# Fourier features kept as 130 mirrored columns instead of 256, and gate rows multiplied out of two fp32r parts instead of fp32

## The reference

```python
def fourier_mixer(h, w_o):
    B, S, D = h.shape
    hg = h.astype(jnp.float32).reshape(B, S, FOURIER_GROUPS, FOURIER_GROUP_DIM)   # 4 groups of 256
    f = jnp.fft.fftn(hg, axes=(1, 3), norm="ortho").real.astype(h.dtype)
    return f.reshape(B, S, D) @ w_o

# second_block, layer i (0: Fourier, 1: retention)
mod = c_act @ w_ada[i] + b_ada[i]
sh1, sc1, g1, sh2, sc2, g2 = jnp.split(mod, 6, axis=-1)
h = modulate(rmsnorm(x, norm_mix_g[i]), sh1, sc1)
x = x + g1[:, None, :] * fourier_mixer(h, w_fourier_out[j])      # or retention_mixer
h = modulate(rmsnorm(x, norm_ffn_g[i]), sh2, sc2)
x = x + g2[:, None, :] * swiglu(h, w_ffn_in[i], w_ffn_out[i])
```

## Time and profile before

| | |
|---|---|
| median of 3 runs | 1161.5 us (1161.35 to 1162.33) |
| the profiled execution's own time | 1163.92 us |
| its span, first to last instruction | 1161.8 us |
| granted TensorE clock, mean | 0.996 |
| TensorE busy | 1144.9 us, 99% |
| VectorE busy | 836.4 us, 72% |
| ScalarE busy | 537.9 us, 46% |
| HBM traffic | 223 GB/s over the span |

### The profile page before, as it was taken

How to read it: one execution, slowest core, us unless ns; L and a number is a source line. 1 busy time by engine, 2 the same in 40 slices (tenths; PEclk the granted TensorE clock), 3 DMA queues, 4 the chain that set the end, 5 groups by cost and what they waited for, 6 DMA issues and landing times.

```text
span 1161.8 us, 14068 instructions
## 1 busy us (share of the span) xinstructions
PE 1144.9 (99%) x5856; PEld 967.3 (83%) x5856; DVE 836.4 (72%) x965; ACT 537.9 (46%) x525; POOL 27.2 (2%) x51
## 2 busy tenths in 40 slices
PE   9999999999999999999999999999999999999997
PEld 7998998888788888888788888889877887888886
DVE  6789879977587668566777676479846857867754
ACT  6656456525553443555544343443332444444431
POOL 1000000000000000000000000000001000000000
PEclk9999999999999999999999999999999999999999
DMA  7854553456477778534367768368743654877751
GB/s 270 309 223 157 187 189 139 162 205 259 145 290 273 270 296 292 199 109 146 145 247 263 293 258 342 131 241 301 291 176 109 246 225 161 308 292 270 287 204 37
DMA packets 39071, 259.81 MB, mean 224 GB/s; under 512 B 4192, under 2 KB 6496, under 8 KB 8416
## 3 DMA queue, kind: packets, MB, share of 16 engines
q1 hardware_dynamic: 37392, 251.84, 58.8%
q0 software_dynamic: 1616, 7.08, 1.8%
HBM read 257.86 MB, written 1.05 MB: 223 GB/s over the span
## 4 chain that ended last, share of the span: by engine, by line
PE 89%; DVE 6%; ACT 2%; DMA 2%; issue 2%; POOL 0%; SPq 0%; POOLq 0%; ACTq 0%; DVEq 0%
PE pair L449 45%; PE pair L514 18%; PE pair L475 10%; PE pair L530 4%; PE tp L571 3%; DVE w_lo L1275 3%; PE tp L633 2%; PE tp L847 1%; DMA raw<-stream 1%; PE pair L786 1%; ACT w_hi L878 1%; PE tp L775 1%; DVE hb L1325 1%; PE tp L660 1%; PE tp L825 1%
## 5 line engine op out<-in xcount | busy, mean ns | idle before, releaser
L1275 DVE TENSOR_TENSOR w_lo<-raw,w_hi 128x2048 fp32r<-128x2048 f32 x180 | 409.2, 2287 | 100.2 <-ACT w_hi L878 99.4
L878 ACT ACTIVATE w_hi<-raw 128x2048 fp32r<-128x2048 f32 x180 | 344.0, 1915 | 224.6 <-DMA raw<-stream 129.7
L449 PE MATMUL pair<-w_hi,ht_lo 128*128 128x512 f32 x800 | 319.5, 399 | 5.8 <-DVE w_lo L1275 5.8
L449 PE MATMUL pair<-w_lo,ht_hi 128*128 128x512 f32 x800 | 312.4, 391 | 0.0
L449 PE MATMUL pair<-w_hi,ht_hi 128*128 128x512 f32 x800 | 312.2, 390 | 0.0
L449 PEld LDWEIGHTS pair<-w_hi,ht_lo 128*128 128x128 f32 x800 | 150.7, 188 | 38.5 <-DVE w_lo L1275 7.5
L449 PEld LDWEIGHTS pair<-w_lo,ht_hi 128*128 128x128 f32 x800 | 150.5, 188 | 32.1
L449 PEld LDWEIGHTS pair<-w_hi,ht_hi 128*128 128x128 f32 x800 | 150.9, 189 | 30.6 <-issue 1.2
L1284 DVE SCALAR_TENSOR_TENSOR raw<-raw,crow 128x1024 f32<-128x1024 f32 x112 | 132.3, 1218 | 0.6 <-DMA raw<-stream 0.6
L514 PE MATMUL pair<-w_hi,gt_lo 128*128 128x512 f32 x272 | 107.5, 395 | 0.5 <-DVE gt_lo L1351 0.3
L514 PE MATMUL pair<-w_lo,gt_hi 128*128 128x512 f32 x272 | 106.0, 390 | 0.0
(11 more groups left out here) (230 smaller groups left out, 1289.9 us busy)
## 6 DMA issues: line engine op xcount, KB each, us to landing
raw<-stream SPq DMA_DIRECT2D x237, 1024.0 KB, 4.9
xres<-x SPq DMA_DIRECT2D x2, 512.0 KB, 4.9
raw<-stream SPq DMA_DIRECT2D x4, 256.0 KB, 7.0
prow<-rows POOLq DMA_DIRECT2D x1, 1024.0 KB, 8.6
xres<-x POOLq DMA_DIRECT2D x2, 512.0 KB, 5.7
dt<-decay POOLq DMA_DIRECT2D x1, 1024.0 KB, 7.0
outT<-outb SPq DMA_DIRECT2D x4, 256.0 KB, 2.6
csr<-dft POOLq DMA_DIRECT2D x1, 768.0 KB, 4.7
```

What stands on the lines that cost most here:

```text
L449: mm = pe.matmul(pair[use % 2][:, t, :], a[:, 4 * c + k, t * P:(t + 1) * P], b[:, w % WS, k * 512:(k + 1) * 512], start=(c == 0 and k == 0 ...
L878: sc.activation(w_hi[:, w % WS, :], raw[:, n % RAW, :], ACT.Copy).then_inc(hi_done, 1)
L1275: v.tensor_tensor(w_lo[:, w % WS, :], raw[:, n % RAW, :], whi32[:, w % WS, :], ALU.subtract).then_inc(raw_done, 1)
```

## The change

Two things change, independent of each other.

**130 of 256 bins.** The input of the feature transform is real, so its cosine sum is the same at bin 256-j as at bin j, and its sine sum has the other sign. `features` now makes bins 0 to 129 of both (`HALF = 130`): the moving operand is two runs of 130 columns out of `cs`, 260 in all, and the copies to `tt_hi` and `tt_lo` are 260 columns wide. `tokens` makes as many matmuls of the same width as before: for m = 0 it takes bins 0 to 127 as stationary operand, for m = 1 bins 1 to 128, read as bins 255 down to 128, and there the sine table enters with the other sign (`cs` from column 256 instead of 512). The second half of each group's mixed features thereby stands in reversed order on the partitions, and the host reverses the rows of `fo` to match (`mirrored`).

**Gate rows in two fp32r parts.** `gate_diagonals` first copies the gate's eight columns to an fp32r tile, subtracts to get the low part (both with a wait on the step before), and writes high and low diagonals with one instruction each of 128 x 1024, whose two inputs are repeated by access pattern. `gate_rows` multiplies the ones, now of type fp32r, with the high and the low diagonals: four fp32r matmuls of 512 columns in place of two fp32 products. The other uses of `ones` stay fp32.

```diff
--- before.py
+++ after.py
@@ -27,6 +27,7 @@
 D = 1024
 KT = D // P
 FF = 2816
+HALF = 130
 FT = FF // P
 HEADS = 8
 HH = HEADS // 2
@@ -200,7 +201,8 @@
         xn = sb("xn", 164, [P, TT, D])
 
         idn = sb("idn", 172, [P, P])
-        ones = sb("ones", 172.5, [P, P])
+        ones_r = sb("ones", 172.5, [P, P], F32R)
+        ones = ones_r[:].bitcast(F32)
         col = sb("col", 173, [P, NCOL])
         mod = sb("mod", 173.875, [P, 112])
         moda = sb("moda", 174.375, [P, 5, 8])
@@ -239,13 +241,14 @@
         prow = sb("prow", 185.25, [P, 2, D])
         praw = sb("praw", 193.25, [P, 2, S])
         pt = [sb("pt_hi", 195.25, [P, 2, S], F32R), sb("pt_lo", 197.25, [P, 2, S], F32R)]
-        dg = sb("dg", 88, [P, KT, P])
-        dgb = sb("dgb", 185.25, [P, KT, P])
+        dg = [sb("dg_hi", 88, [P, KT, P], F32R), sb("dg_lo", 92, [P, KT, P], F32R)]
+        dgb = [sb("dgb_hi", 185.25, [P, KT, P], F32R), sb("dgb_lo", 189.25, [P, KT, P], F32R)]
+        modr = sb("modr", 174.3125, [P, 2, KT], F32R)
         prod = sb("prod", 92, [P, 2, TT, 256])
         csr = sb("csr", 112, [P, 2, 768])
         cs = [sb("cs_hi", 185.25, [P, 2, 768], F32R), sb("cs_lo", 191.25, [P, 2, 768], F32R)]
         grow = [sb("grow0", 201.25, [P, D]), sb("grow1", 197.25, [P, D])]
-        tt = [sb("tt_hi", 112, [P, TT, 4, 512], F32R), sb("tt_lo", 134, [P, TT, 4, 512], F32R)]
+        tt = [sb("tt_hi", 112, [P, TT, 4, 2 * HALF], F32R), sb("tt_lo", 134, [P, TT, 4, 2 * HALF], F32R)]
         qr = sb("qr", 112, [P, RH, 2, S])
         kr = sb("kr", 120, [P, RH, 2, S])
         vr = sb("vr", 128, [P, TT, RH * RV])
@@ -590,8 +593,11 @@
                 for half in range(2):
                     k = JOB[name] + half
                     claim(k)
-                    pe.matmul(tp[k % BANKS][:], ones[:], dg[:, 4 * half:4 * half + 4, :].rearrange("p a b -> p (a b)"),
-                              start=True, stop=True).then_inc(tp_done, 1)
+                    for part in range(2):
+                        mm = pe.matmul(tp[k % BANKS][:], ones_r[:],
+                                       dg[part][:, 4 * half:4 * half + 4, :].rearrange("p a b -> p (a b)"),
+                                       start=(part == 0), stop=(part == 1))
+                    mm.then_inc(tp_done, 1)
 
             def hidden(name, jobs, j):
 
@@ -772,7 +778,9 @@
                     claim(k)
                     for d in range(2):
                         for n, (a, b) in enumerate(passes(ht, cs)):
-                            mm = pe.matmul(tp[k % BANKS][:], a[:, 2 * gr + d, t * P:(t + 1) * P], b[:, d, 0:512],
+                            mm = pe.matmul(tp[k % BANKS][:, 0:2 * HALF].rearrange("p (a b) -> p a b", a=2),
+                                           a[:, 2 * gr + d, t * P:(t + 1) * P],
+                                           b[:, d, 0:2 * S].rearrange("p (a b) -> p a b", a=2)[:, :, 0:HALF],
                                            start=(d == 0 and n == 0), stop=(d == 1 and n == 2))
                     mm.then_inc(tp_done, 1)
 
@@ -784,8 +792,8 @@
                         for part in range(2):
                             for o, (a, b) in enumerate(passes(tt, cs)):
                                 mm = pe.matmul(mixed(gr)[:, m * S:(m + 1) * S],
-                                               a[:, t, gr, part * S + m * P:part * S + (m + 1) * P],
-                                               b[:, t, 2 * part * S:(2 * part + 1) * S],
+                                               a[:, t, gr, part * HALF + m:part * HALF + m + P],
+                                               b[:, t, (2 - m) * part * S:((2 - m) * part + 1) * S],
                                                start=(t == 0 and m == 0 and part == 0 and o == 0),
                                                stop=(t == 1 and m == 1 and part == 1 and o == 2))
                     if t:
@@ -1155,7 +1163,9 @@
 
             def dft_his(name, t, groups):
                 for gr in groups:
-                    hi(JOB[name] + gr, tt[0][:, t, gr, :])
+                    k = JOB[name] + gr
+                    act.wait_ge(tp_done, k + 1)
+                    hi(k, tt[0][:, t, gr, :], tp[k % BANKS][:, 0:2 * HALF])
 
             for t in range(TT):
                 if t == 0:
@@ -1390,8 +1400,12 @@
             def gate_diagonals(at_col, read=None, dg=dg):
                 if read is not None:
                     dve.wait_ge(tp_done, read)
-                for m in range(KT):
-                    ins = v.tensor_scalar(dg[:, m, :], idn[:], mod[:, at_col + m:at_col + m + 1], None, ALU.mult)
+                gate = mod[:, at_col:at_col + KT]
+                link(v.tensor_copy(modr[:, 0, :], gate))
+                link(v.tensor_tensor(modr[:, 1, :], gate, as_f32(modr[:, 0, :]), ALU.subtract))
+                for part in range(2):
+                    ins = v.tensor_tensor(dg[part][:], idn[:].unsqueeze(1).to_broadcast([P, KT, P]),
+                                          as_f32(modr[:, part, :]).unsqueeze(2).to_broadcast([P, KT, P]), ALU.mult)
                 ins.then_inc(dg_done, 1)
 
             def hidden_los(jobs, j):
@@ -1691,7 +1705,7 @@
             def dft_los(name, t, groups):
                 for gr in groups:
                     k = JOB[name] + gr
-                    lo(k, tt[1][:, t, gr, :], tt32[:, t, gr, :], tp[k % BANKS][:])
+                    lo(k, tt[1][:, t, gr, :], tt32[:, t, gr, :], tp[k % BANKS][:, 0:2 * HALF])
 
             for t in range(TT):
                 wait_evac(dve, USE["pleg"] + t)
@@ -1885,6 +1899,11 @@
 
         return w.T.reshape(-1, 2, P, D).transpose(0, 2, 1, 3).reshape(-1, P, 2 * D)
 
+    def mirrored(w):
+
+        a = w.reshape(-1, 2, P, D)
+        return np.stack([a[:, 0], a[:, 1, ::-1]], axis=1).reshape(D, D)
+
     def outer(w):
         return w.reshape(-1, 2, P, D).transpose(0, 2, 1, 3).reshape(-1, P, 2048)
 
@@ -1901,7 +1920,7 @@
         "zi": deep(z["zi"], 512), "zg": deep(z["zg"], 512), "ga": deep(z["ga"], 512), "gb": deep(z["gb"], 512),
         "wa": outer(get("w_a")[0]), "wb": outer(get("w_b")[0]), "wout": outer(get("w_out")[0]),
         "ffn0": gate_up(get("w_gate")[0], get("w_up")[0]), "down0": outer(get("w_down")[0]),
-        "ple": outer(get("w_ple")[0]), "pleg": outer(get("w_ple_gate")[0]), "fo": outer(get("w_fourier_out_2")[0]),
+        "ple": outer(get("w_ple")[0]), "pleg": outer(get("w_ple_gate")[0]), "fo": outer(mirrored(get("w_fourier_out_2")[0])),
         "ffn1": gate_up(fi[0][:, :FF], fi[0][:, FF:]), "down1": outer(fo[0]),
         "rq": deep(ri[:, 0:1024], 256), "rk": deep(ri[:, 1024:2048], 256),
         "rva": deep(ri[:, 2048:3072], 512), "rvb": deep(ri[:, 3072:4096], 512), "rg": deep(ri[:, 4096:6144], 512), "ro": outer(get("w_ret_out_2")[0]),
```

## The result

The changed kernel takes 1155.52 us in the median of 4 runs (1154.07 to 1156.12), the kernel before 1161.42 us (1161.29 to 1162.33): a ratio of 0.9946, 95% interval 0.9928 to 0.9963. Forecast were 1154.9 us and a range of 1153.0 to 1158.0. The profiled execution took 1156.12 us with a span of 1154.0; the one of before took 1163.92 and 1161.8.

The account below looks back on a forecast made before the run. TensorE was taken as the bound, busy 1144.9 of 1161.8 us, with VectorE close behind in the Fourier stage. Fourier stage 4.2 plus three sets of gate rows 2.4 gave 6.6 us off 1161.5: 1154.9 us, range 1153.0 to 1158.0.

Parts of the forecast that it names:

- 3, transposes of tile 1: Fourier stage: TensorE waits 0.3 us for the norm, then transposes tile 1 from 522.05 instead of 524.1.
- 4, VectorE scales tile 1: Fourier stage: scaling starts 1.9 us earlier, at 522.75, so tile 1 is ready at 527.6 instead of 529.51.
- step 1: `features` of tile 0: three groups take 2.5 us, no stall for the first low part, fourth group ends at 518.8.
- step 6: `features` of tile 1 starts at 527.6, its fourth group runs to 530.95; `tokens` of tile 1 gains 4.2 us.
- Step 7: `tokens` of tile 1: fourth low part ready at 535.2, needed at 535.27; `fo` starts at 536.8, gain 4.2 us.
- step 5: After the first gate rows TensorE waits about 1 us for tile 1's split; the 0.81 us of `rows0` is worth nothing.
- (a): `features`: cost of a moving operand in two runs of 130; taken as 0.122 us, from above 0.43.
- (b): 48 of 96 `tokens` matmuls: stationary operand one column off; taken as costing nothing, from above 5.1 us.
- The rivals that hung on them: In `features`, short runs lose the fp32r rate: 1168.5 us, chance 0.04; in `tokens`, shifted weights are dearer: 1160.0, chance 0.05.
- that of the diagonals: Rival at the four gate-row places: VectorE's dearer diagonals reach the path, up to 4.8 us back, 1155 to 1159.7; chance 0.03.
- full payout: Rival in the Fourier stage: nothing is absorbed, 5.0 us there, 1153.3 us in all; chance 0.06.
- the greater absorption: Rival: thin margins miss or copies gain less, Fourier stage gives only 2 to 3 us, 1156 to 1157.5; chance 0.09.

Follow-up runs that it names:

- rows_only: Kernel before with only the gate rows in two fp32r parts, 256 bins kept: 1159.87 us, ratio 0.9978.
- rows0_fp32: Changed kernel with the first set of gate rows put back to fp32 products and eight diagonals: 1154.19 us, ratio 0.9932.
- fourier_only: Kernel before with only the 130-bin part of the change, gate rows left in fp32: 1158.56 us, ratio 0.9969.
- diagonals_twice: Changed kernel with each pair of diagonals written twice on VectorE: 1154.9 us, ratio 0.9933.
- changed_again: The changed kernel itself, unaltered, timed again on another chip: median 1154.2 us, ratio 0.9934.
- keep_busy: Changed kernel with eight small fp32 products filling a 2.3 us TensorE wait in the first feed-forward layer: median 1154.03 us, ratio 0.9928.

## Why the prediction was right

Times relative to the start of the first `features`, as predicted and as measured:

| step | predicted | measured |
|---|---|---|
| 1, TensorE's stall ahead of the fourth group | none | 0.19 |
| 1, fourth group starts | 2.48 | 2.48 |
| 3, transposes of tile 1 | 6.48 | 6.40 |
| 4, VectorE scales tile 1 | 7.18 | 7.09 |
| 5, TensorE's wait behind the gate rows | 1 us | 0.69 (0.87 from start to start) |
| 6, second `features` | 12.03 | 11.96 |
| 6, its fourth group | 14.63 | 14.50 |
| 6, `tokens` of tile 1 | 15.38 | 15.33 |
| 7, gain of the stage | 4.2 | 4.31 |

- **The prices** held: 0.122 us for 260 columns (measured 0.122), 0.39 and 0.42 us for the copies (0.39 and 0.42 to 0.43), 0.91 for the gate rows (0.91 and 0.92), 1.22 for a diagonal (1.22 to 1.23).
- **Two errors cancelled in steps 1 and 6.** The prediction gave each `features` some 0.3 us at its start, out of the chain's sums. TensorE's records show 0.10 more than the pace there (0.22 from the first start to the second), and the rest is a stall ahead of the fourth group, for the first low part: 0.19 us at tile 0, where step 1 says "No stall", and 0.26 at tile 1 (529.83 against 529.57 by the pace), where step 6 has 0.1. The start of the fourth group came out right because VectorE sets it. Step 7 had more room than its 0.07 us: the fourth low part ends at 534.20 + 0.42 = 534.62, and TensorE starts on the last group at 534.95.
- **What step 5 said of `rows0`** was shown by three runs: nothing when cheapened alone (`rows_only`, 0.05 us), nothing when put back (`rows0_fp32`, 0.01 us), nothing missing in `fourier_only`.
- **The unknown costs** (a) two short runs and (b) the shifted stationary operand both came out at their lower bound, 0.122 and 0.119 us. The rivals that hung on them are out, that of the diagonals too (`diagonals_twice`), and the stage's 4.31 us lie between full payout (5.0) and the greater absorption (2 to 3).
- **The sum** of 6.6 us is 0.7 more than the first set's medians give and 1.2 less than the profiled executions' 7.8. Of these 7.8 the Fourier stage has 4.31 and three sets of gate rows 2.42; 0.24 lies ahead of the first `features`. The remaining 0.8 is the end of the program, which no step of mine has. From the last piece of the chain, a copy by ScalarE, to the end of the span it is 1161.8 - 1158.22 = 3.6 us before and 1154.0 - 1151.21 = 2.8 after, and the stores of the result take longer from issue to landing. The last piece of the chain and, from the list of transfers, the row of the stores (its last column is the median in us from issue to landing), before and then changed:

```profile
1157.52 0.70 ACT outb L910 x2
...
outT<-outb SPq DMA_DIRECT2D x4, 256.0 KB, 2.6
```

```profile
1150.51 0.70 ACT outb L918 x2
...
outT<-outb SPq DMA_DIRECT2D x4, 256.0 KB, 2.3
```

- **That end goes with the gate rows' part, as far as the traces tell.** It is 3.35 us in `fourier_only`, whose gate rows are those of before, and 2.6 to 2.9 in the eleven other traces, which have at least three sets of the new ones, `rows_only` among them. The two long ones alone have a packet of the instruction queue among the stores. Whether that packet is the cause, no run tests, so the cause stays open.
- **The distance between 6.6 and the medians' 5.9 is the clock, and that 1154.9 came so close to 1155.52 is in part luck.** I took the median's distance from the profiled time as a constant of 2.4 us, where some 1.5 us of it comes and goes with the clock. The first set's median of before (1161.42) lies where its executions at a mean clock of 0.998 lie, that of the changed kernel (1155.52) among those at 0.997; against `changed_again` it is the other way round, 1162.4 - 1154.2 = 8.2 us. With like against like on that chip, the means are 1161.44 and 1154.10 us for executions at 0.998 or 0.999, and 1162.75 and 1155.69 at 0.997: the change gives 7.1 to 7.3 us. In the same way, against means of before of 1161.36 and 1162.98 us on their chip, `fourier_only` gives 4.2 us (six executions at 0.997) and `rows_only` 3.0 (nine at 0.996 or 0.997) and 3.1 (one at 0.998). The steps have 4.3 and 2.4 for them. By these means the half microsecond that the sum lacks is in the gate rows' part, not in the Fourier stage.

## What to carry to other kernels

When an engine is 99% busy and two chains meet at one point, count a saving ahead of that point only as far as the other chain shrinks too: here 3.1 us saved by TensorE ahead of the second `features` (2.3 in the first `features`, 0.8 in the gate rows) moved it by 2.0, from 13.99 to 11.96 us behind the start of the first. A wait that appears after such a change can be taken back only if everything that ends with it is moved: either of two reorderings gave 0 to 0.14 us, both together 1.1. And compare edits under 1 us by intervals within the trace, from one fixed event to another; whole executions of this kernel differ by some 1.5 us for a reason far from the edit, and the medians of two kernels can fall into different clusters.

## What the hardware showed unasked

- An fp32r matmul falls from 0.227 us at 512 columns to 0.122 at 260 along the line of the columns, but only to 0.111 at 192, where that line has 0.094. If 0.111 is a floor, which one width can't show, narrowing below about 234 columns is worth nothing at these stationary operands (an estimate: where the line through 0.227 and 0.122 meets 0.111).
- A moving operand in two runs of 130 columns, and a stationary one that starts one column off, cost no more than the pace of whole ones: 0.122 us, which the line through 512 and 256 columns gives for 260, and 0.119 against 0.120.
- One TensorE wait of 2.3 us brought the clock to its lower level in some executions of the same program and not in others (it fell in eight of the twelve traces with this wait), and cost 1.4 to 1.6 us. With eight products into an unused bank, 1.8 us of work in that wait, the clock stayed up in the two traces that have them; the other four executions of `keep_busy` show it only by their times, all under 1154.3 us, and a mean clock of 0.998.
